# Two-block network on one core: the first mixer's mask in parts, and five moves of work in the recurrent mixer

## The reference, cut to what matters

```python
def sgu_mixer(h, w_in, b_in, g_v, w_s, b_s, w_out):
    z = jax.nn.gelu(h @ w_in + b_in, approximate=False)
    u, v = jnp.split(z, 2, axis=-1)
    v = rms_norm(v, g_v)
    ...
    w_causal = jnp.where(causal[None], w_s, 0)           # 16 groups of 128 x 128
    v = jnp.einsum('gts,bnsgc->bntgc', w_causal, v) + b_s.T[None, None, :, :, None]
    return (u * v.reshape(B, S, SGU_HALF)) @ w_out

def wkv7_scan(r, w, k, v, a, b):
    def step(state, inp):                                 # 16 heads of 64 x 64
        r_t, w_t, k_t, v_t, a_t, b_t = inp
        sa = jnp.einsum('bhvk,bhk->bhv', state, a_t)
        state = (state * w_t[:, :, None, :] + sa[..., None] * b_t[:, :, None, :]
                 + v_t[..., None] * k_t[:, :, None, :])
        y_t = jnp.einsum('bhvk,bhk->bhv', state, r_t)
        return state, y_t
    ...

def rwkv7_mixer(...):
    ...
    y = wkv7_scan(r_h, decay, k_h, v_h, -kk, kk * a_h)
    mean = jnp.mean(y, -1, keepdims=True)
    var = jnp.mean(jnp.square(y - mean), -1, keepdims=True)
    y = ((y - mean) * lax.rsqrt(var + GN_EPS)).reshape(B, S, D)
    y = y * ln_w.astype(f32) + ln_b.astype(f32)
    bonus = jnp.sum(r_h * k_h * r_k.astype(f32), -1, keepdims=True) * v_h
    y = (y + bonus.reshape(B, S, D)).astype(h.dtype)
    return (y * g) @ w_o
```

## Time and profile before

| what | us |
|---|---|
| median of 3 runs | 2907.25 |
| lowest and highest run | 2893.02, 2907.39 |
| the profiled execution | 2909.55 |
| its span in the trace | 2907.7 |
| PE busy | 2779.8 (96%) |
| DVE busy | 1527.9 (53%) |
| ACT busy | 1059.4 (36%) |
| POOL busy | 779.3 (27%) |

### The profile page before, as it was taken

The page is one execution under the profiler, slowest core; times in us unless marked ns, Lnnn a source line. Parts: engine busy times, 40 slices in busy tenths (PEclk is TensorE's granted clock), DMA queues, the critical chain, the costliest instruction groups (busy, mean ns, idle before and its releaser), DMA issues. The chain is left out here.

```text
span 2907.7 us, 37500 instructions
## 1 busy us (share of the span) xinstructions
PE 2779.8 (96%) x13734; PEld 2211.1 (76%) x13734; DVE 1527.9 (53%) x1889; ACT 1059.4 (36%) x1868; POOL 779.3 (27%) x710
## 2 busy tenths in 40 slices
PE   8999999799899999999999888899999999999999
PEld 6888888557798778888677766588888756788887
DVE  4477762644643577774467555653433346644432
ACT  5333332334333433333255445422222247422221
POOL 3231112440812531112102535221111135411100
PEclk9999999899898999999999889999999999999999
DMA  4222233211100023223222021132233310122333
GB/s 148 79 95 94 95 91 96 89 44 58 52 1 19 1 88 100 94 91 95 85 87 80 15 61 43 39 104 95 94 93 95 100 53 1 58 94 94 101 86 103
DMA packets 80539, 218.96 MB, mean 75 GB/s; under 512 B 21917, under 2 KB 22045, under 8 KB 80158
## 3 DMA queue, kind: packets, MB, share of 16 engines
q1 hardware_dynamic: 79262, 215.17, 23.8%
q10 hardware_dynamic: 1152, 2.10, 0.2%
HBM read 215.14 MB, written 2.10 MB: 75 GB/s over the span
## 5 line engine op out<-in xcount | busy, mean ns | idle before, releaser
L311 PE MATMUL psum<-rounded,high_r 128*128 128x512 f32 x3040 | 1205.5, 397 | 45.6 <-PEq L120 11.0
L313 PE MATMUL psum<-rounded,high_r 128*128 128x512 f32 x3040 | 1191.2, 392 | 0.0
L315 PE MATMUL psum<-rounded,ring_low 128*128 128x512 f32 x3040 | 1190.4, 392 | 0.0
L331 ACT ACTIVATE high_r<-ring 128x1024 fp32r<-128x1024 f32 (+2 forms) x432 | 420.4, 973 | 1409.3 <-PE psum L315 1388.8
L336 DVE TENSOR_TENSOR ring_low<-ring,high_r 128x1024 fp32r<-128x1024 f32 (+2 forms) x430 | 526.8, 1225 | 566.1 <-ACT high_r L331 564.8
L311 PEld LDWEIGHTS psum<-rounded,high_r 128*128 128x128 f32 x3040 | 575.9, 189 | 203.4 <-issue 48.2
L315 PEld LDWEIGHTS psum<-rounded,ring_low 128*128 128x128 f32 x3040 | 575.5, 189 | 121.9
L313 PEld LDWEIGHTS psum<-rounded,high_r 128*128 128x128 f32 x3040 | 576.3, 190 | 118.5 <-issue 1.4
L769 DVE TENSOR_TENSOR arena<-psum,inverse 128x512 f32<-128x512 f32 x176 | 121.5, 691 | 314.3 <-PE psum L315 314.2
L624 POOL CAST rounded<-rows 128x512 f32 (+1 forms) x88 | 53.9, 613 | 785.4 <-DVE rows L774 785.4
L626 POOL TENSOR_TENSOR rounded<-rows,rounded 128x512 f32 (+1 forms) x88 | 115.6, 1313 | 13.2 <-POOL rounded L624 11.9
(11 more groups left out here) (413 smaller groups left out, 2985.7 us busy)
## 6 DMA issues: line engine op xcount, KB each, us to landing
ring<-in_up SPq DMA_DIRECT2D x176, 512.0 KB, 3.3
ring<-in_down SPq DMA_DIRECT2D x64, 384.0 KB, 3.1
ring<-in_down SPq DMA_DIRECT2D x64, 320.0 KB, 2.9
ring<-in_even_in SPq DMA_DIRECT2D x36, 512.0 KB, 3.7
ring<-in_sgu_in SPq DMA_DIRECT2D x16, 512.0 KB, 3.5
ring<-in_even_out SPq DMA_DIRECT2D x16, 384.0 KB, 3.1
ring<-in_qkv SPq DMA_DIRECT2D x12, 512.0 KB, 3.7
ring<-in_sgu_out SPq DMA_DIRECT2D x8, 512.0 KB, 3.3
```

The source lines that it names most:

```text
L311: nc.tensor.matmul(psum[:, m, :], high_r[:, r % HIGHS, blk], x_high, start=(k0 + k == 0), stop=False)
L313: nc.tensor.matmul(psum[:, m, :], high_r[:, r % HIGHS, blk], x_low, start=False, stop=False)
L315: mm = nc.tensor.matmul(psum[:, m, :], ring_low[:, r % R, blk], x_high, start=False, stop=end)
L331: nc.scalar.activation(high_r[:, r % HIGHS, 0:nk * P], ring[:, r % R, 0:nk * P], ACT.Copy).then_inc(unit_high, 1)
```

## The change

The first mixer's mask is cut in four parts of four groups, each behind a Gelu, between POOL's squares. In the recurrent mixer the scores of unit 0 and their masks go from behind unit 6 of the v product to behind unit 4, and the pairs 4 to 7 one place back each (units 5 and 6); ACT's copies and the spread follow. Pairs 4 and 5 wait for the masks, since they write the same PSUM banks. The turn back of unit 5 goes behind the last round's addition. `bonus_sums` goes behind the output's matmuls. `keep_state` adds in PSUM and multiplies out of it. At the end `gate_rest(0)` goes into unit 15, before its last round, ACT keeps the first four gates before the last y, DVE gates three outputs before the last norm, `gate(4)` goes ahead of `turn_output(3)`, and the two low weight parts go from POOL to DVE (in unit 15 and last of all).

```diff
-                    nc.gpsimd.tensor_tensor(wcv, wcv, con("le").unsqueeze(1).to_broadcast([P, NH, P]), ALU.mult).then_inc(masked, 1)
+                    pool.wait_ge(taken, 1)
                     for i in range(KD):
+                        if i < 4:
+                            part = wcv[:, 4 * i:4 * i + 4, :]
+                            nc.gpsimd.tensor_tensor(part, part, con("le").unsqueeze(1).to_broadcast([P, 4, P]), ALU.mult).then_inc(masked, 1)
                         pool.wait_ge(taken, i + 1)
...
+                        if n in (4, 5):
+                            pe.wait_ge(masked, 2 * (n - 3))
...
                     def score(u, step):
                         if u == 0:
-                            pe.wait_ge(diagonal_kept, 8 * BLOCKS)
+                            pe.wait_ge(diagonal_kept, 4 * BLOCKS)
+                            pe.wait_ge(hat_steps, 6 * (KD - 1) + 1)
+                            pe.wait_ge(powered, KD)
...
-                        elif n < 6:
-                            pair_of_units(2 * n - 4)
-                            pair_of_units(2 * n - 3)
-                        elif n == 6:
+                        elif n == 4:
                             score(0, 0)
                             score(0, 1)
+                        elif n < 7:
+                            pair_of_units(2 * n - 6)
+                            pair_of_units(2 * n - 5)
...
-                        if u in (8, 9):
-                            bonus_sums(u - 8)
...
+                        if u in (8, 9):
+                            mm = bonus_sums(u - 8)
                         mm.then_inc(y_done, 1)
...
                         turn_keys(u)
-                        if more and not changes(u):
+                        if not more:
+                            gate_rest(0)
+                        elif not changes(u):
                             carry(u + 1)
                         round_of(u, 2)
...
                     output(UNITS - 1)
-                    gate_rest(0)
-                    for i in range(4):
+                    for i in range(3):
                         turn_output(i)
-                    for n in range(4, KD):
+                    gate(4)
+                    turn_output(3)
+                    for n in range(5, KD):
                         gate(n)
...
-                    keep_y(UNITS - 1)
                     for m in range(4):
                         keep_gate(m)
+                    keep_y(UNITS - 1)
+                    output_high(0)
                     root(4)
+                    for i in range(1, 4):
+                        output_high(i)
                     split_high(act, Stream("rwkv_o"), 0, 1)
-                    for i in range(4):
-                        output_high(i)
...
+                        if n == 4:
+                            for k in range(4):
+                                mask(0, k)
                         if n == 6:
                             dve.wait_ge(diagonal_kept, 8 * BLOCKS)
                             turn_in(1).then_inc(turned_in, 1)
-                            for k in range(4):
-                                mask(0, k)
...
-                                nc.vector.tensor_tensor(s0, new, s0, ALU.add).then_inc(s_added, 1)
+                                nc.vector.tensor_tensor(new, new, s0, ALU.add).then_inc(s_added, 1)
                                 dve.wait_ge(s_added, 2 * additions_before(u) + e + 1)
-                                nc.vector.tensor_tensor(s0, s0, sc, ALU.mult).then_inc(s_kept, 1)
+                                nc.vector.tensor_tensor(s0, new, sc, ALU.mult).then_inc(s_kept, 1)
...
                             invert(3)
+                            split_low(dve, Stream("rwkv_o"), 0, 0)
...
+                        keep_round(u, 2)
                         if u == 5:
                             dve.wait_ge(steps1, SUBSTITUTED)
                             turn_back(1).then_inc(turned_back, 1)
-                        keep_round(u, 2)
...
+                    for i in range(3):
+                        gate_output(i)
                     variance(4, UNITS)
                     invert(4)
...
                     output_low(KD - 1)
+                    split_low(dve, Stream("rwkv_o"), 0, 1)
...
-                    weights_low(0)
                     whiten(3)
                     pool.wait_ge(y_done, UNITS)
                     nc.gpsimd.tensor_tensor(v_of(4), v_of(4), spread_over(bonus, 4), ALU.mult).then_inc(last_bonus, 1)
-                    weights_low(1)
```

31 lines of the change are left out of this document (17 added, 14 removed).

## The result

The changed kernel takes 2884.78 us (median of 8 runs, 2872.31 to 2888.07), beside 2908.02 us before (8 runs, 2893.02 to 2910.34): a ratio of 0.9913, with a 95% interval of 0.9896 to 0.993. The forecast was 2885, with a range of 2872 to 2899. The profiled execution took 2885.85 us with a span of 2884.0.

A forecast was written before the change was run, and what follows sets the result against it. The matmul engine PE, busy for 96% of the span, was taken as the bound; gains of 21.9 us gave 2887.6 for the profiled execution, and 2885 as it lay 2.3 above the median; range 2872 to 2899.

The forecast's parts named there:

- mask: First mixer: mask in four parts removes PE's 3.90 us wait; gain 2.2 us, bounds 0.5 to 2.9.
- end of v products: Before the recurrence: first scores fill PE's 6.08 us wait, first carry comes earlier; gain 5.0 us, bounds 3.5 to 5.7.
- unit 0's clock: Unit 0 of the recurrent mixer: new wait may bring the low clock; up to 5 us either way, taken as 0.
- turn back: Unit 5: transpose moved behind the last round's addition, into DVE's idle time; gain 1.3 us, bounds 0.8 to 1.4.
- bonus sums: Unit 9: no wait before the sums, gain 1.6 us, and no low clock, gain 8.3 us, bounds 0 and 9.
- state in PSUM: Unit 11: state's product reads PSUM, so POOL no longer holds it; gain 3.0 us with clock, bounds 0 to 3.2.
- end of mixer: Last norm: POOL's weight subtraction goes to DVE, against new work on the path; gain 0.5 us, bounds -2 to +2.
- rival (2): DVE's PSUM step still waits for POOL, or the tail meets POOL's subtractions; 2890.5 us with both; chance 0.11.
- rival (1): Clock stays low in unit 9, as the wait's role was only inferred; 2893.3 us; chance 0.19.
- rival (4): Better than forecast: both low stretches go; 2880 us; chance 0.05.

The follow-up runs named there:

- sums ahead again: Changed kernel with the bonus sums of units 8 and 9 put back ahead of the output's 16 small matmuls: 2885.76 us (5 runs).
- sums one unit later: Kernel before with the bonus sums still ahead of the output's matmuls but in units 9 and 10: 2889.95 us, ratio 0.9943.
- the second set: Changed kernel timed again, unchanged, beside the three edits and the kernel before, six runs each: 2888.09 us, ratio 0.9926.
- sums behind only, second time: Kernel before with only the bonus sums moved behind the output's matmuls, run again for another trace: 2902.52 us, ratio 0.9981.

## Why the prediction was right, by its steps

The terms, forecast and measured between the points of the first table (before less after):

```
mask, to the first mixing product           2.2     0.93
end of v products, pairs to carry(0)        5.0     4.85   (80.77 to 75.92)
unit 0's clock, carry(0) to carry(2)        0      -0.45   (27.47 to 27.92)
turn back, carry(6) to carry(7)             1.3     1.56   (12.12 to 10.56)
bonus sums, carry(9) to carry(11)           9.9    10.99   (36.30 to 25.31)
state in PSUM, carry(11) to carry(14)       3.0     3.65   (40.54 to 36.89)
end of mixer, carry(15) to first output     0.5     0.71   (30.09 to 29.38)
elsewhere                                   0       1.45
sum                                        21.9    23.69
```

*Mask.* The mechanism was right (the wait for DVE goes, two waits for ACT's gains come), the size was not: 0.93 for 2.2, within its bounds. The clock fell at the new waits (the turn of 1.11 us), which I had counted as the unlikely case; at the second turn the changed kernel was still 2.6 us ahead (33.37 for about 35.97), and 1.7 of that was gone at the mixing. The sum also passed over that the row of before already held a fall of its own, behind the wait of 3.90. The runs show that this place differs by 2 to 3 us between executions of one code.

*End of the v products.* Right to 0.2 us, with the wait of 2.24 for 2.5. The carry itself is at 779.57 for 780.6, because 1.2 us had been won ahead of the pairs. What I called late next (the last pairs, copies, two transposes and the spread) is what PE waited for; that ACT's copy of the product ends nearly as late was not seen.

*Unit 0.* Taken at 0 with 5 either way. In the pair of profiles it is 0.45; over all traces it comes and goes: low in 8 of 14, with 7.3 us between the two (carry(0) to carry(2) 27.92 in the changed kernel, 20.59 with the sums ahead again). That the wait before the first carry brings it is not shown: a wait of 2.0 to 2.2 us stands there in four traces that are low and in five that are not, and of the five traces with the old order, which have no wait of PE there, four are low. What the fall does go with is the start of the stage against the grid of the clock's changes (above); why is open.

*Turn back, state, end of the mixer.* Each near what was worked out, the first two for the stated reasons: the transpose of 1.99 now lies in idle time, the product of 0.29 shows that a step with an input in PSUM isn't held, and the hold in the norm moved from one step to others. Of the rival (2) the first half didn't come (no held step in PSUM), and the second did (the norm meets POOL's subtractions); by the Trainium skill's rule alone the sum there would have been near -1, and it is 0.71. The hold itself has grown, from 2.0 us to 2.7, so that from carry(15) the norm ends 0.5 later than before (26.5 us for 26.0). What outweighs it lies behind the norm and is in no part of the sum: PE's last turn of outputs starts 0.1 us behind the norm's last step and not 0.8, and it takes 1.94 us at a clock of 1.00, where before it took 3.56 at 0.50. So this term came out near its 0.5 by luck. That the state's term needs its collision was not foreseen: in the kernel with the sums one unit later it isn't there in SBUF form either.

*Bonus sums.* The largest term, taken in full, was right in its place (10.99 for 9.9) and its cause is shown: four of four traces with the wait have the slow unit 9, none of ten without it has, and of these one has the matmuls in the old order. It is shown for the one place of the grid where all four stand. The rival (1) falls for the profiled executions. What was not right is the step from a stage to the whole time. Put back or taken out by itself, this part moved the medians by 1, 5 and 8 us and, in the kernel in which unit 0 was high, by 12. In the five runs with the sums ahead again none reached the 2892 or so that both low stretches together would give, and all five have the mean granted clock of the profiled one, 0.976 to 0.977. Either unit 0 was high in all five, or unit 9 was spared in those in which it was low, with the wait at another place of the grid. The second would also fit the 1, 5 and 8 us, which are less than the stage's 11. Only one of the five has a trace, so this stays open.

The sum came out right (21.9 for 23.7) with the mask too large by 1.3 and four others too small by 0.2 to 1.1 each, and the median fell on the forecast partly by luck: the changed kernel's runs lie at 2872, at 2877 and around 2885, and in the second set around 2888. Those three of the eight that took 2872 to 2877 had a mean granted clock of 0.980 or 0.981, the five others 0.976 or 0.977; the fast three are below the 2880 of rival (4). Of the 1.45 us won elsewhere, 1.2 lie behind the first output product, where nothing was changed. The lower end of the range was added up a little wrong: the bounds named there give 2876.4 and not 2875, and the upper ones 2898.3; neither matters here.

## What to carry to other kernels

Look for waits of one or two microseconds at places where the matmuls are few and small: the idle time is the least of it, the clock behind it cost more than five times as much here (1.6 of idle time, 9.4 of clock), and it is got rid of by putting work that is ready ahead of the work that waits. Judge a small edit by the stage it touches, in several traces: the medians of four to ten runs were 7 to 11 us away from what the stage showed, and gains by medians didn't add. Where two engines meet on SBUF, a new schedule moves the hold; ask which instruction stands in it next, and let one of them wait on purpose.

## What was not expected of the hardware

- A wait of 1.64 us was enough to bring PE to the 1.2 GHz level for nearly the whole of unit 9 (22.38 to 22.65 us at 0.58 to 0.59, in four traces), and waits of 2.24, 0.93 and 0.71 us elsewhere in some executions brought nothing. The fall came just over 1 us behind the end of the wait (before: PE goes on at 900.81, the clock is 1.00 from 901 to 902 and 0.50 from 902.5).
- Behind the mixer, where no code was changed, the stretch from the first output product to the end took between 1888.6 us (sums ahead again) and 1896.1 us (sums behind only, second time) in the profiled executions: 7.5 us. By the clock's record in the traces the first spent 69 us of it at the 1.2 GHz level and the second 84, and over all fourteen traces the time of this stretch goes with its time at that level, about 0.43 us for each microsecond. Why more of it is low in one execution than in another was not followed up.
- The instruction that gets SBUF first keeps it: with 0.01 us between the two starts it was once DVE's 1.22 us that went through and POOL's 4.94 that became 5.67, and in other executions POOL's 4.94 that went through and DVE's two that took 6.68.
- Not only instructions with two inputs in SBUF are held: a step of eight elements a row (`variance`, free 0.17 us) took 2.89 us beside POOL. It ended within 0.05 us of POOL's addition of 4.53 us, which had begun ahead of it, and PE had no wait for it. The timeline of the kernel after, in unit 12:

```profile
940.61 2.89 DVE L1945 TENSOR_SCALAR small<-small 128x8 f32<-128x8 f32 x1
```
